# Attention scores on half of TensorE's rows per map, in a one-core decoder step

## The reference

```
xn = rms_norm(h);  qa,ka,va,qb,kb,vb,ga,gb = split(xn @ w_in)          # 512 x6, 1024 x2
A (4 heads; q = q1|q2, k = k1|k2 of 64 each, v of 128):
   p = softmax(q1 k1'/8 + bias) - lam * softmax(q2 k2'/8 + bias);  o_a = p v
B (8 heads of 64, keys strictly before the query):
   z = q k'/8;  a[t,s] = sigmoid(z_ts) * prod_{s<j<t} (1 - sigmoid(z_tj));  o_b = a v
h += (sigmoid(ga) * (norm(o_a) @ w_pa) + sigmoid(gb) * (o_b @ w_pb)) @ w_out
PEER: q = rms_norm(h) @ w_q; scores against sub-keys; 8 heads x 16 experts per token;
   h += sum over the 128 experts of gate * gelu(xn . u[expert]) * v[expert]
y = rms_norm(h)
```

## Time and profile before

| | |
|---|---|
| timed runs | 3628.34, 3624.38, 3628.4 us; median 3628.34 |
| profiled execution | 3612.7 us, its span 3610.8 us |
| busy, share of the span | PE 79%, DVE 74%, POOL 63%, ACT 26% |
| read from HBM | 1323.53 MB, 374 GB/s over the span |
| mean granted TensorE clock | 0.926 |
| records of L1314 | 384 of MATMUL, first at 171.1 us, last at 2724.4 us |
| first score of turns 0 to 7, us | 171.1, 362.7, 733.5, 1142.0, 1506.7, 1860.7, 2225.4, 2592.3 |

### The profile page before, as it was taken

The page is one execution under the profiler, slowest core; times in us unless marked ns, Lnnn a source line. Parts: engine busy times, 40 slices in busy tenths (PEclk is TensorE's granted clock), DMA queues, the critical chain, the costliest instruction groups (busy, mean ns, idle before and its releaser), DMA issues.

```text
span 3610.8 us, 28652 instructions
## 1 busy us (share of the span) xinstructions
PE 2837.2 (79%) x7810; PEld 1289.1 (36%) x7810; DVE 2663.1 (74%) x5556; ACT 931.7 (26%) x1845; POOL 2280.3 (63%) x2214
## 2 busy tenths in 40 slices
PE   7999978987897667777777778877787777767756
PEld 5644433333342333343334333433343323323211
DVE  4314887898787868897788778967897766568775
ACT  5322311222122312232224222422242223312110
POOL 0100565677667767777777677766777665456776
PEclk9999989999898899989998999899999988889978
DMA  7543999999999999999999999999999999999998
GB/s 237 204 138 128 345 417 418 408 395 409 418 406 385 386 414 418 413 390 415 419 406 373 404 419 409 366 409 419 406 366 408 412 405 358 345 342 404 419 402 355
DMA packets 401335, 1353.32 MB, mean 375 GB/s; under 512 B 47347, under 2 KB 51571, under 8 KB 400026
## 3 DMA queue, kind: packets, MB, share of 16 engines
q0 software_dynamic: 315616, 1148.34, 80.3%
q1 hardware_dynamic: 62162, 163.81, 12.2%
q10 hardware_dynamic: 23400, 39.35, 3.0%
HBM read 1323.53 MB, written 27.80 MB: 374 GB/s over the span
## 4 chain that ended last, share of the span: by engine, by line
POOL 25%; PE 24%; DMA 21%; issue 12%; DVE 11%; ACT 2%; SPq 0%; DVEq 0%; ACTq 0%
POOL t_ring L1255 25%; DMA t_ring<-in_peer_v,t_idx 10%; PE ps L1344 7%; PE ps L1492 7%; DMA t_ring<-in_peer_u,t_idx 6%; PE ps L1508 6%; DVE t_ring L2060 4%; DVE t_acc L2081 3%; DMA t_big<-in_w_out 2%; DMA t_big<-in_peer_w_query 2%; PE ps L1283 1%; DMA keyT<-in_cache_k_sb 1%; ACT t_pTr L1535 1%; DVE t_big L1832 1%; PE ps L1460 1%
## 5 line engine op out<-in xcount | busy, mean ns | idle before, releaser
L1508 PE MATMUL ps<-t_ring,t_diag 128*128 128x512 f32 (+1 forms) x2472 | 1303.9, 656 | 431.4 <-DMA t_ring<-in_peer_v,t_idx 406.7
L2060 DVE CUSTOM_DVE_ANT_0 t_ring<-t_ring,ps 128x1024 f32<-128x1024 f32 x1088 | 1318.7, 1216 | 384.3 <-DMA t_ring<-in_peer_u,t_idx 377.2
L1255 POOL DMA_INDIRECT t_ring<-in_peer_u,t_idx x1088 | 1120.6, 1030 | 748.7 <-issue 278.4
L1255 POOL DMA_INDIRECT t_ring<-in_peer_v,t_idx x1088 | 1142.7, 1050 | 422.4 <-issue 273.9
L1508 PEld LDWEIGHTS ps<-t_ring,t_diag 128*128 128x128 f32 (+1 forms) x2472 | 452.5, 200 | 1162.8 <-DMA t_ring<-in_peer_v,t_idx 743.1
L2081 DVE SCALAR_TENSOR_TENSOR t_acc<-t_ring,t_wgt,t_acc 128x1024 f32<-128x1024 f32 x469 | 603.4, 1287 | 114.7 <-DMA t_ring<-in_peer_v,t_idx 104.2
L1492 PE MATMUL ps<-val,keyT 128*128 128x512 f32 x800 | 382.0, 615 | 29.7 <-DMA val<-in_w_in 21.7
L1344 PE MATMUL ps<-t_big,t_pTr 128*128 128x512 f32 x696 | 345.6, 641 | 64.9 <-DVE t_big L1854 19.5
L1700 ACT ACTIVATE t_diag<-ident,t_wgt 128x128 f32<-128x128 f32 x583 | 222.8, 398 | 514.5 <-PE ps L1508 483.0
L1535 ACT COPY t_pTr<-ps 128x512 f32<-128x512 f32 (+3 forms) x216 | 110.5, 512 | 570.2 <-PE ps L1283 569.0
L1344 PEld LDWEIGHTS ps<-t_big,t_pTr 128*128 128x128 f32 x696 | 136.1, 204 | 263.4 <-issue 147.3
(11 more groups left out here) (228 smaller groups left out, 2157.1 us busy)
## 6 DMA issues: line engine op xcount, KB each, us to landing
t_big<-in_peer_w_query SPq DMA_DIRECT2D x72, 512.0 KB, 7.9
t_big<-in_w_out SPq DMA_DIRECT2D x65, 512.0 KB, 7.9
wraw<-in_w_in SPq DMA_DIRECT2D x40, 512.0 KB, 5.2
val<-in_w_in ACTq DMA_DIRECT2D x40, 512.0 KB, 9.3
t_ring<-in_peer_u,t_idx POOLq DMA_INDIRECT x1088, 7.6
t_ring<-in_peer_v,t_idx POOLq DMA_INDIRECT x1088, 7.6
t_big<-in_w_proj_sb SPq DMA_DIRECT2D x19, 512.0 KB, 11.0
proj_d<-val ACTq DMA_DIRECT2D x36, 256.0 KB, 5.9
```

The source lines that it names most:

```text
L1255: pool.indirect_dma_start(row(kind, e, s), None, table, bass.IndirectOffsetOnAxis(ap=idx[:, e % 2, s:s + 1], axis=0)).then_inc(s_ring[g % ...
L1508: m = nc.tensor.matmul(ps[0:n, c, :], diag[:, v_place[e, s] % NDG, 0:n], row("v", e, s)[:, c * CH:(c + 1) * CH], start=v_first(e, s), stop ...
L2060: nc.vector.tensor_tensor_reduce(out=row("u", e, s), in0=row("u", e, s), in1=x_row, scale=1.0, scalar=0.0, op0=ALU.mult, op1=ALU.add, accu ...
```

## The change

- ACT copies a group of queries once, with the constant factor 0.125, into `qT_all`, one slot where there were two. `half_scale` and the four fills that set it are gone.
- A score is a product over the 64 partitions of its map alone: `qT_all[rows, u, :]` against `keyT[rows, u, ...]`, rows 0 to 63 for map 0 and 64 to 127 for map 1. The number of matmuls and their columns stay.
- Where a score is a single matmul (turns 0 to 3) both maps of a head are issued one after the other at the beat of map 0; nothing is issued at the beat of map 1. Each keeps its own waits and its own semaphore. In turns 4 to 7 the beats stay.

```diff
-        half_scale = keep("half_scale", [P, 2])
...
-                        for m in range(2):
-                            nc.vector.memset(half_scale[64 * m:64 * m + 64, m:m + 1], 0.125)
-                            nc.vector.memset(half_scale[64 * m:64 * m + 64, 1 - m:2 - m], 0.0)
...
-            qz = slots(9, 11).rearrange("p (u m r) -> p u m r", m=2, r=P)
+            qT_all = big[:, 9, :].rearrange("p (u r) -> p u r", r=P)
...
                 for c in range(0, kw, CH):
                     wide = min(CH, kw - c)
-                    m = nc.tensor.matmul(scores_of(t, hf)[:, c:c + wide], qz[:, u, hf, :], keyT[:, u, c:c + wide],
+                    rows = slice(64 * hf, 64 * hf + 64)
+                    m = nc.tensor.matmul(scores_of(t, hf)[:, c:c + wide], qT_all[rows, u, :], keyT[rows, u, c:c + wide],
                                          start=True, stop=True)
...
                 elif kind == "scores":
-                    pe_scores(pe, t, *which)
+                    u, hf = which
+                    if width(t) > CH:
+                        pe_scores(pe, t, u, hf)
+                    elif hf == 0:
+                        pe_scores(pe, t, u, 0)
+                        pe_scores(pe, t, u, 1)
...
-                    nc.scalar.activation(qz[:, 4 * g:4 * g + 4, 0, :], src, ACT.Copy, scale=half_scale[:, 0:1])
-                    act_T.raised_by(nc.scalar.activation(qz[:, 4 * g:4 * g + 4, 1, :], src, ACT.Copy, scale=half_scale[:, 1:2]))
+                    act_T.raised_by(nc.scalar.activation(qT_all[:, 4 * g:4 * g + 4, :], src, ACT.Copy, scale=0.125))
```

## The result

The kernel after takes **3689.4 us** (median of five runs, 3684.1 to 3697.2) against 3628.3: ratio **1.0176, 95% interval 1.016 to 1.0191**. It is 61 us slower by the medians, 64 by the ratio; the forecast was 3629 and its range ended at 3644. The profiled execution took 3684.1 us, with a span of 3682.1 against 3610.8.

A forecast was written before the change was run, and what follows sets the result against it. PE was taken to bound until about 418 us, the DMA engines being near full after. Turn 0 +0.9, turn 1 -0.8, turns 2 and 3 0, turns 4 to 7 +1.2: together +1.3, so 3629 us, range 3616 to 3644.

The forecast's parts named there:

- Smaller ones: First stage: four fills of half_scale go while PE and the stores hold that stage open, 0.
- What bounds: PE bounds from 163 to 418 us; after that the DMA share is near 1.0 and PE has idle time.
- The height changes in turns 4 to 7: 16 visits per turn at 0.42 us, 27 us of PE in all, mostly hidden: +1.2 at the end, bounds 0 to +27.
- POOL waits for PE under 2 us: Sign for turns 4 to 7: POOL's waits for PE stay under 2 us; several us would show the forecast wrong.
- PE's waits for gathered rows: Sign for turns 4 to 7: these waits get shorter by about 6 us in each turn.
- half of it: Slower rival: half the full price of height changes in turns 4 to 7 reaches the end, 3642; height changes had chance 0.13.
- Turns 0 to 3: One visit per head with both maps: +1.6, -0.1, -1.8, -3.5 us of PE per turn; turns 2 and 3 counted 0.
- the overlap: Turns 0 to 3: a head's two half-height matmuls run side by side; rival without overlap 3635, chance 0.05.
- the added wait: A head's pair waits for VectorE's take of the previous head's second map: 0, bounds 0 to +2.2 us.
- ScalarE's copies: One copy for two, 16 times, 0.7 us less each: -0.5 in turn 0, -0.7 in turn 1, later 0, at best -4.2.
- The gates: Turn 0: the gates' load is released some 4 us earlier; ScalarE stood 3.20 us before the sigmoid: -0.2 us.
- The clock: Slower rival: half-height work brings more low-clock stretches, 20 us over four turns, 3648, chance 0.08; sign: clock below 0.85.

The follow-up runs named there:

- e8: Kernel before, addresses kept, with 64 rows for each map in turns 4 to 7 alone: ratio 1.0025 (1.0014 to 1.0036).
- e2: Kernel before without the unused tile aside, so tiles from keyT on take the addresses of the kernel after: ratio 1.0148 (1.0128 to 1.0168).
- e10: Kernel before plus a half-height matmul of 64 columns ahead of each of a score's two chunks in turns 4 to 7: ratio 1.0045 (1.0028 to 1.0061).
- e11: Kernel before at full height, addresses kept, with one ScalarE copy of the queries for two, maps not separated: ratio 0.9984 (0.9969 to 0.9999).
- e7: Kernel before, addresses kept, with the score change in turns 0 to 3 alone, two copies staying: ratio 1.0007 (0.9995 to 1.0018).
- e4: Kernel before with pads around the gathers' ring, so that it alone stands 32 bytes off a multiple of 256: 3657.2 us, ratio 1.0111 (1.0088 to 1.0135).

## Why the prediction was wrong

**The step that failed** is the one in "Smaller ones": the fills of `half_scale` go, 0. It looked at the tile's instructions and not at its bytes. The 32 bytes carried every later tile to a multiple of 256; without them the transfers into these tiles take longer (shown by itself for the ring alone), and from turn 1 on the DMA engines have no slack for it. That costs 1.0134 to 1.0148, 49 to 54 us. No rival of mine had it, since all of them asked what an instruction does. That the addresses move could have been worked out, since the sizes are in the declarations; what a remainder costs, no row of the trace of before shows.

**What bounds** was read rightly, and for that reason the loss is so large: a transfer that takes 2% longer costs nothing in turn 0 (DMA share 0.2 to 0.6) and comes through where the share is 1.

**The height changes in turns 4 to 7** were mis-sized twice. A visit is 0.3 us, not 0.42 (my 0.32 from the sub-key scores already held most of the entering and leaving), so 64 x 0.3 = 19 us of PE, not 27. And half height there costs 9 us at the end (5 to 13, e8), not 1.2, by the visits or in part by the clock: I took the idle time in one stretch of turn 6 for cover in four turns. Those rows still look so after:

```profile
POOL t_ring L1251 <- issue: 25.9, 85, 0.3
...
POOL t_ring L1251 <- PE ps L1510: 0.7, 2, 0.4
```

so the tell "POOL waits for PE under 2 us" held while the kernel lost, and in the scores of turns 4, 5 and 7 too (0.3, 0 and 0.6 us). PE's waits for gathered rows, foretold about 6 us shorter in each, went from 20.0, 20.0, 12.5 and 10.6 us to 19.4, 13.3, 10.7 and 10.0. From 418 us to the end POOL waits longer for PE's additions; before, after, and e1, the change with the old addresses:

```profile
POOL t_ring L1255 <- PE ps L1508: 213.8, 133, 11.2
```

```profile
POOL t_ring L1251 <- PE ps L1510: 276.7, 230, 12.6
```

```profile
POOL t_ring L1252 <- PE ps L1511: 223.8, 156, 11.9
```

But this comes with the addresses, not with the height: e2, with not one instruction changed, has 274.1 us. With the old addresses the wait is no measure of the loss: 213.3 us in e10, which is slower, and 234.9 in e11, which is not.

With the old addresses the change comes to 1.0041, 3643 us on the median's scale: the number of the rival "half of it", 3642, given 0.13, and not the forecast's. That it is so near is in part luck, since half height in turns 4 to 7 brings 9 of the 15 us. So the forecast of no change was wrong even without the addresses, by 14 us.

**Turns 0 to 3**: the overlap held; by 0.1 + 0.2 for a visit the four turns' PE time changes by +0.6, -1.0, -2.8 and -4.5 us (an estimate from these prices). That it doesn't reach the end held as well (e7). The earlier trace rows show the two records of one matmul, not two matmuls on the same rows; that two such matmuls don't overlap shows in turn 4, where the first score after, two matmuls on one half, holds PE for 1.27 us and held it for 1.08 before. In the added wait PE stood longer than I thought, 5.2 us in six waits, 4.4 of them in turns 0 to 3; in e7 (4.7 us in five) it cost nothing that can be told:

```profile
  issue: 79.6, 209
  DVE t_mx L1776: 5.2, 6
```

**ScalarE's copies**: the copy takes 0.60 us, and in turn 0 PE begins its next transposes 0.65 us after the copy's start, where it was 1.32.

```profile
165.42 0.60 ACT L1562 ACTIVATE t_big<-ps 128x512 f32<-128x512 f32 x1 [5.47 <-PE ps L1279]
...
166.07 1.11 PE L1279 MATMUL ps<-ident,gain_fin 128*128 128x128 f32 x4 [0.69 <-ACT t_big L1562]
```

The sum's -1.2 is inside the interval of e11, and so is the bound of -5.4, which lies nearer to its middle. **The gates**: the sigmoid no longer waits for its load but for PE, 1.84 us where it stood 3.20:

```profile
226.20 1.91 ACT L1602 ACTIVATE t_big<-t_big 128x2048 f32<-128x2048 f32 x1 [1.84 <-PE ps L1494]
```

Turn 1's first score is at 363.4, within the 1 us foretold, but that is luck: turn 0 itself is 0.3 us shorter, and the first score of turn 0 alone lies anywhere from 169.3 (e1) to 173.2 us (e4). **The clock** in the scores of turns 4 to 7 stayed above the 0.85 that I named, at 0.88, 0.88, 0.87 and 0.89, where it was 0.89, 0.91, 0.88 and 0.92; over the whole span it is 0.916 against 0.926.

**Open.** The parts, measured alone, add up to 0.07 + 0.25 - 0.16 = 0.16%, the whole (e1) to 0.41%; the intervals together are +-0.27%, so it isn't shown whether the parts act on each other. How much of the 15 us the clock carries is open too. Why a transfer takes longer off the multiple isn't shown; only the tiles in SBUF were moved.

## What to carry to other kernels

Removing or adding a tile, however small, is an edit of every address behind it: work the addresses out before and after, and keep DMA destinations on multiples of 256 bytes where the DMA engines bound. A transfer ceiling that comes down at the same DMA share, in stages that the edit doesn't touch as well, points at the whole program's layout and not at the edited instructions. A matmul of 64 rows among neighbours of 128 cost 0.3 us here for the way there and back, so it pays only where what it saves is more than that and PE bounds.

## What the runs showed of the hardware

Destinations in SBUF 32, 128, 192 or 224 bytes past a multiple of 256 all cost about the same: 1.011 for the ring alone at 32, 1.012 to 1.015 for all tiles at the others, with the fullest slices at 410 GB/s (414 for the ring alone) in place of 419 or 420, and 4 KB gathers landing after 8.2 to 8.5 us in place of 7.4 to 7.6. Two fp32 matmuls of 64 rows on the two halves start together (0.007 us apart) with 128 to 512 columns, and the pair takes one map's time and 0.20 us up to the next matmul of full height.
